# Row sums with the ones held still, a first root in two parts, high parts ahead of gate copies, and GpSimd scaling the last attention's probabilities

## What is computed

```python
# layer 0 and 1 of the first block: mod = silu(c) @ ada_w[i] + ada_b[i], six sections of 1024 each
h  = modulate(rmsnorm(x, norm1_g[i]), sh1, sc1)       # x*(1+sc1)+sh1
# layer 0: differential attention, 8 heads of 128, keys of context and x together (512)
p  = softmax(s[0]) - lam_full * softmax(s[1]);  o = p @ v
o  = rmsnorm(o, subln_g) * (1 - lam_init);      y = o.reshape(256, 1024) @ wo
# layer 1: short convolution
b_gate, c_gate, u = split(h @ w_in, 3);         y = (b_gate * conv3(c_gate * u)) @ w_out
# after each mixer: x = x + g1*y ; x = x + g2 * swiglu(modulate(rmsnorm(x), sh2, sc2))
# second block, layer 2: neighbourhood attention; layer 3: latent attention, 16 heads
pr = softmax(q @ k.T * 96**-0.5);  o = pr @ v;  y = (o * silu(z)) @ w_out
x  = h + sigmoid(rmsnorm(h) @ ple_w_gate) * (p @ ple_w_proj);  return rmsnorm(x, final_norm)
```

## Time and profile before

| what | value |
|---|---|
| time, median of 3 runs | 1090.65 us (1090.09 to 1091.9) |
| time of the profiled execution | 1092.87 us |
| span of its records | 1090.8 us |
| busy: TensorE matmul, weight load | 95%, 88% |
| busy: VectorE, ScalarE, GpSimd | 72%, 47%, 0% |
| mean granted TensorE clock | 0.982 of 2.4 GHz |

### The profile page before, as it was taken

The page is one execution under the profiler, slowest core; times in us unless marked ns, Lnnn a source line. Parts: engine busy times, 40 slices in busy tenths (PEclk is TensorE's granted clock), DMA queues, the critical chain, the costliest instruction groups (busy, mean ns, idle before and its releaser), DMA issues.

```text
span 1090.8 us, 18302 instructions
## 1 busy us (share of the span) xinstructions
PE 1035.3 (95%) x7740; PEld 960.9 (88%) x7740; DVE 790.3 (72%) x1184; ACT 509.4 (47%) x732; POOL 0.7 (0%) x6
## 2 busy tenths in 40 slices
PE   4899999799999999998999999999999999999895
PEld 2689875699999999998999999999987998997684
DVE  3689759668787887887986646568746568896665
ACT  3623238454434344424343444445347665457562
POOL 0000000000000000000000000000000000000000
PEclk9899999899999999999999999999999999999898
DMA  9769541038998987566746676564754053543130
GB/s 367 273 214 330 187 174 39 2 104 291 318 302 293 316 284 245 189 226 233 248 155 209 208 242 213 175 191 129 232 182 162 2 184 119 185 138 150 37 119 38
DMA packets 118592, 210.14 MB, mean 193 GB/s; under 512 B 4250, under 2 KB 82288, under 8 KB 118512
## 3 DMA queue, kind: packets, MB, share of 16 engines
q1 hardware_dynamic: 117764, 206.81, 55.9%
q10 hardware_dynamic: 748, 2.18, 0.5%
HBM read 207.92 MB, written 1.05 MB: 192 GB/s over the span
## 4 chain that ended last, share of the span: by engine, by line
PE 79%; DVE 12%; ACT 3%; issue 2%; DMA 1%; SPq 1%; DVEq 0%; ACTq 0%
PE PS L1625 12%; PE PS L1626 12%; PE PS L1627 12%; PE PS L1710 8%; PE PS L1729 8%; PE PS L1711 8%; DVE low L998 3%; PE PS L1636 3%; PE PS L1748 2%; PE PS L1749 2%; PE PS L1753 2%; PE PS L1843 1%; PE PS L1844 1%; DMA ada_raw<-in_ada_w 1%; PE PS L1916 1%
## 5 line engine op out<-in xcount | busy, mean ns | idle before, releaser
L998 DVE TENSOR_TENSOR low<-raw,high 128x2048 fp32r<-128x2048 f32 (+2 forms) x147 | 328.1, 2233 | 153.5 <-ACT high L585 153.1
L585 ACT ACTIVATE high<-raw 128x2048 fp32r<-128x2048 f32 (+2 forms) x147 | 273.1, 1866 | 226.0 <-PE PS L1627 111.2
L1710 PE MATMUL PS<-hH,high 128*128 128x258 f32 x896 | 221.8, 284 | 4.6 <-ACT high L585 1.9
L1711 PE MATMUL PS<-hL,high 128*128 128x258 f32 x896 | 220.3, 283 | 0.0
L1710 PEld LDWEIGHTS PS<-hH,high 128*128 128x128 f32 x896 | 169.8, 189 | 6.5 <-issue 2.9
L1711 PEld LDWEIGHTS PS<-hL,high 128*128 128x128 f32 x896 | 168.7, 188 | 0.1
L1729 PE MATMUL PS<-hH,low 128*128 128x258 f32 x896 | 126.3, 283 | 0.3
L1729 PEld LDWEIGHTS PS<-hH,low 128*128 128x128 f32 x896 | 115.6, 189 | 1.3 <-DVE low L998 1.3
L1625 PE MATMUL PS<-gH,high 128*128 128x256 f32 x352 | 98.5, 280 | 0.0
L1626 PE MATMUL PS<-gL,high 128*128 128x256 f32 x352 | 98.4, 280 | 0.0
L1627 PE MATMUL PS<-gH,low 128*128 128x256 f32 x352 | 98.2, 279 | 0.0
(11 more groups left out here) (325 smaller groups left out, 1945.8 us busy)
## 6 DMA issues: line engine op xcount, KB each, us to landing
raw<-in_ffn_w_in SPq DMA_DIRECT2D x44, 1024.0 KB, 6.4
ada_raw<-in_ada_w SPq DMA_DIRECT2D x82, 512.0 KB, 5.4
raw<-in_ffn_w_out SPq DMA_DIRECT2D x22, 1024.0 KB, 6.0
raw<-in_na_w_in SPq DMA_DIRECT2D x16, 1024.0 KB, 5.5
raw<-in_da_wqkv SPq DMA_DIRECT2D x12, 1024.0 KB, 8.8
raw<-in_sc_w_in SPq DMA_DIRECT2D x12, 1024.0 KB, 5.7
...
```

The source lines that it names most:

```text
L585: nc.scalar.activation(high[s][:, 0:width(u)], raw[s][:, 0:width(u)], ACT.Copy).then_inc(high_ready, 1)
L998: V_.tensor_tensor(low[s][:, 0:w], raw[s][:, 0:w], high[s][:, 0:w].bitcast(F), ALU.subtract).then_inc(low_dve, 1)
L1710: MM(PS[:, b + c, 0:SEQ + 2], high[s][w(j, c)], hH[:, j, 0:SEQ + 2], start=j == 0, stop=False)
L1711: MM(PS[:, b + c, 0:SEQ + 2], high[s][w(j, c)], hL[:, j, 0:SEQ + 2], start=False, stop=False)
```

## The change

1. **Sections 0 and 1**: `ada_acc` is turned by plain transposes, eight for each section into two banks (4, 5 and 6, 7), and one VectorE `tensor_reduce` for each adds the four tiles' rows. `sel2` goes.
2. **Sections 2 to 11**: the 32 columns of ones are stationary and 256 columns of `ada_acc` move, in four column tiles (four matmuls). ScalarE copies the 128x256 result to `sum_rows` (the tile `wide[3]`; `copy_rows`), and behind the next input unit TensorE turns it with two transposes (`turn_rows`) into bank 7, 5 or 6; VectorE takes it there (`section_turned`).
3. **The first root**: heads of rounds 0 to 11 are rooted in three steps inside rounds 13, 14 and 15, their blocks scaled, turned and split ahead of the rest; the last block of four heads follows, and TensorE turns it behind the first output unit. `newton` is split into `root_guess`, `root_series` and `root_closed`, the operations being the same.
4. **The convolution's input**: ScalarE calls `behind` of unit 3j before it waits for the gate copy.
5. **The last attention**: ScalarE's `gated_high` comes ahead of the exponentials; VectorE keeps the reciprocals, and GpSimd does the 32 scalings.

Left out of the diff: declarations of semaphores, `sel2`, and the splitting of `newton`.

```diff
@@ -187,6 +187,13 @@
+def rows_bank(u, first):
+
+    if u < first["ffn0"]:
+return 7
+    return 6 if first["sc_in"] <= u < first["ffn1"] else 5
@@ -563,6 +573,11 @@
     nc.gpsimd.memset(cond[:, :, :], 0.0).then_inc(consts_ready, 1)
+    for h in range(16):
+        pool.wait_ge(sums_inverted, h + 1)
+        for t in range(TT):
+            ins = nc.gpsimd.tensor_scalar(E2[:, h % 4, t, :], E2[:, h % 4, t, :], rsum[:, 2 * h + t:2 * h + t + 1], None, ALU.mult)
+        ins.then_inc(probs_scaled, 1)
@@ -586,6 +601,12 @@
+
+    def copy_rows(u):
+
+        if u in reduce_at:
+            seen.next(rows_made)
+            nc.scalar.activation(sum_rows[:, :], bank(7, SEQ), ACT.Copy).then_inc(rows_copied, 1)
@@ -662,6 +683,7 @@
         behind(first["da_q"] + j)
+        copy_rows(first["da_q"] + j)
     def da_exp(i):
@@ -677,6 +699,7 @@
             nc.scalar.activation(V[:, tt, 512 * nb:512 * nb + 512], bank(V_BANK[nb][tt]), ACT.Copy).then_inc(vz_copied, 1)
+        copy_rows(ua + 1)
         behind(ua + 1)
@@ -721,6 +744,7 @@
             ua = u0 + (3 * i - 1 if i else 0)
+            copy_rows(ua)
             seen.next(a_taken)
@@ -741,13 +765,14 @@
         u = first["sc_in"] + 3 * j
+        behind(u)
         seen.next(c_taken)
...
         ins.then_inc(c_copied, 1)
-        behind(u)
         behind(u + 1)
         behind(u + 2)
+        copy_rows(u + 2)
         act.wait_ge(conv_staged, j + 1)
@@ -918,11 +943,11 @@
         turned(2 * p + 1)
+        if p % 2 == 0 and p:
+            gated_high(p // 2 - 1)
         if p + 2 < 8:
...
             exps(2 * p + 5, False)
-        if p % 2 == 0 and p:
-            gated_high(p // 2 - 1)
     behind(first["mla_kvb"] + 2)
@@ -977,18 +1002,30 @@
-    def section(g):
-
+    turning = []
+
+    def section(u):
+
+        turning.append((reduce_at[u], rows_bank(u, first)))
+
+    def section_turned():
+
+        if not turning:
+            return
+        g, b = turning.pop()
         layer, part = divmod(g, 6)
...
         sections_done[0] += 1
-        b = cols[:, NROWS + 8 * g:NROWS + 8 * g + 8]
+        by_column = "p (j h) -> p j h"
+        src = bank(b, SEQ).rearrange("p (h j m) -> p j h m", h=2, j=4)[:, :, :, 0]
+        here = mod[:, g, :].rearrange(by_column, h=2)
+        beta = cols[:, NROWS + 8 * g:NROWS + 8 * g + 8].rearrange(by_column, h=2)
         if part in (SCALE1, SCALE2):
             at, _ = ROWS["norm1_g" if part == SCALE1 else "norm2_g"]
-            link(V_.scalar_tensor_tensor(mod[:, g, :], bank(7, KC), 1.0, b, ALU.add, ALU.add))
+            link(V_.scalar_tensor_tensor(here, src, 1.0, beta, ALU.add, ALU.add))
             V_.tensor_tensor(mod[:, g, :], mod[:, g, :], cols[:, at + 8 * layer:at + 8 * layer + 8], ALU.mult).then_inc(section_taken, 1)
         else:
-            V_.tensor_tensor(mod[:, g, :], bank(7, KC), b, ALU.add).then_inc(section_taken, 1)
+            V_.tensor_tensor(here, src, beta, ALU.add).then_inc(section_taken, 1)
@@ -998,8 +1035,9 @@
     def sections(u):
+        section_turned()
         if u in reduce_at:
-            section(reduce_at[u])
+            section(u)
@@ -1083,7 +1131,10 @@
         b = cols[:, NROWS + 8 * g:NROWS + 8 * g + 8]
-        src = PS[:, (7, 0)[g], 0:16].rearrange("p (c m) -> p m c", m=2)
+        four_rows = PS[:, 4 + 2 * g:6 + 2 * g, :].rearrange("p b (c j m) -> p (b c) m j", c=4, j=4)[:, :, 0:2, :]
+        src = (nwt, var)[g][:, 0:16].rearrange("p (c m) -> p c m", m=2)
+        link(V_.tensor_reduce(src, four_rows, AX.X, ALU.add))
+        src = src.rearrange("p c m -> p m c")
         if g == 0:
@@ -1174,31 +1225,50 @@
+    def da_scaled(t, b):
+        heads = XN[:, t, 512 * b:512 * b + 512].rearrange("p (h e) -> p h e", h=4)
+        k = 8 * t + 4 * b
+        V_.tensor_tensor(heads, heads, rst[:, k:k + 4].unsqueeze(2).to_broadcast([P, 4, P]), ALU.mult).then_inc(xn_ready, 1)
+
+    def da_low(t, b):
+        sl = (slice(None), slice(4 * b, 4 * b + 4), slice(t * P, (t + 1) * P))
+        direct_low(oL[sl], oH[sl], GROUP_BANK[2 * t + b], cols[:, at:at + 1])
...
     da_max(2)
+    section_turned()
     for i in range(16):
...
             da_max(i + 3)
+        if i == 13:
+            v.wait_ge(sq_ready, 12)
+            link(V_.tensor_scalar(var[:, 0:12], ssq[:, 0:12], 1.0 / P, EPS, ALU.mult, ALU.add))
+            root_guess(var[:, 0:12], rst[:, 0:12], nwt[:, 0:12])
+        if i == 14:
+            root_series(nwt[:, 0:12], poly[:, 0:12])
+        if i == 15:
+            root_closed(rst[:, 0:12], nwt[:, 0:12], poly[:, 0:12])
+            da_scaled(0, 0)
+            da_scaled(1, 0)
         seen.next(made_v)
...
             split(first["da_v"] + 3 + RING)
+    da_scaled(0, 1)
+    da_low(0, 0)
+    da_low(1, 0)
     v.wait_ge(sq_ready, 16)
-    inverse_root(0, 16, P)
-    for t, b in BY_HALF:
-        heads = XN[:, t, 512 * b:512 * b + 512].rearrange("p (h e) -> p h e", h=4)
-        k = 8 * t + 4 * b
-        V_.tensor_tensor(heads, heads, rst[:, k:k + 4].unsqueeze(2).to_broadcast([P, 4, P]), ALU.mult).then_inc(xn_ready, 1)
-    for t, b in BY_HALF:
-        sl = (slice(None), slice(4 * b, 4 * b + 4), slice(t * P, (t + 1) * P))
-        direct_low(oL[sl], oH[sl], GROUP_BANK[2 * t + b], cols[:, at:at + 1])
+    inverse_root(12, 16, P)
+    da_scaled(1, 1)
+    da_low(0, 1)
+    da_low(1, 1)
@@ -1549,10 +1620,7 @@
         seen.next(exp_ready)
-        link(V_.reciprocal(rsum[:, 2 * h:2 * h + 2], esum[:, 2 * h:2 * h + 2]))
-        for t in range(TT):
-            ins = V_.tensor_scalar(E2[:, h % 4, t, :], E2[:, h % 4, t, :], rsum[:, 2 * h + t:2 * h + t + 1], None, ALU.mult)
-        ins.then_inc(probs_scaled, 1)
+        V_.reciprocal(rsum[:, 2 * h:2 * h + 2], esum[:, 2 * h:2 * h + 2]).then_inc(sums_inverted, 1)
@@ -1636,21 +1704,37 @@
+    turning = []
+
+    def turn_rows():
+
+        if not turning:
+            return
+        b = rows_bank(turning.pop(), first)
+        seen.next(rows_copied)
+        claim(b)
+        transposes(b, [(h * P, P, sum_rows[:, h * P:(h + 1) * P]) for h in range(2)]).then_inc(section_made, 1)
+        owed(section_taken, b)
...
+        turn_rows()
         if u not in reduce_at:
...
         claim(7)
-        owed(section_taken, 7)
-        for c in range(KC):
-            last = MM(PS[:, 7, c:c + 1], ada_acc[g % 2][:, c * P:(c + 1) * P], ones[:, 0:1], start=True, stop=True)
-        last.then_inc(section_made, 1)
-
-    def output_groups(s, order):
-
-        seen.n[split_low.name + "/freed"] = seen.n[split_low.name]
+        for j in range(4):
+            last = MM(PS[32 * j:32 * j + 32, 7, 0:SEQ], ones[:, 0:32], ada_acc[g % 2][:, j * SEQ:(j + 1) * SEQ],
+                      start=True, stop=True, tile_position=(0, 32 * j))
+        last.then_inc(rows_made, 1)
+        owed(rows_copied, 7)
+        turning.append(u)
+
+    def output_groups(s, order, first_of=True):
+
+        if first_of:
+            seen.n[split_low.name + "/freed"] = seen.n[split_low.name]
         for t, b in order:
@@ -1819,15 +1903,13 @@
     for g in range(2):
-        b = (7, 0)[g]
-        pe.wait_ge(acc_copied, g + 1)
-        claim(b)
-        for c in range(KC):
-            if c == 4:
-                pe.wait_ge(acc_half, g + 1)
-            last = MM(PS[:, b, 2 * c:2 * c + 2], ada_acc[g][:, c * P:(c + 1) * P], sel2[:, :], start=True, stop=True)
+        for n in range(2):
+            b = 4 + 2 * g + n
+            pe.wait_ge((acc_copied, acc_half)[n], g + 1)
+            claim(b)
+            last = transposes(b, [(c * P, P, ada_acc[g][:, (4 * n + c) * P:(4 * n + c + 1) * P]) for c in range(4)])
         last.then_inc(section_made, 1)
-        owed(section_taken, b)
+        owed(section_taken, b - 1, b)
@@ -1916,17 +1999,19 @@
         owed(o_taken, 7)
-    output_groups(xn_ready, BY_HALF)
-
-    def feature_out(u0, per_unit):
+    output_groups(xn_ready, BY_HALF[:3])
+
+    def feature_out(u0, per_unit, last_group=False):
         for k in range(4):
+            if last_group and k == 1:
+                output_groups(xn_ready, BY_HALF[3:], False)
             if per_unit[k]:
...
-    feature_out(first["da_out"], (2, 0, 2, 0))
+    feature_out(first["da_out"], (2, 0, 2, 0), True)
```

18 lines of the change are left out of this document (13 added, 5 removed).

## The result

| what | before | changed |
|---|---|---|
| median of the runs timed together (4 each) | 1091.07 us | 1065.99 us (1065.78 to 1067.14) |
| ratio, 95% interval | | 0.9773 (0.9756 to 0.979) |
| profiled execution, span | 1092.87, 1090.8 us | 1066.09, 1064.3 us |

The changed kernel is 25.1 us faster; 24.3 were forecast, 1066.4 against 1066.0. That it came so close is partly luck: of the five terms one rested on a wrong reason, and inside it a gain of 4.8 us and a loss of 2.3, neither of them forecast, made up nearly the 3.0 that were.

A forecast was written before the change was run, and what follows sets the result against it. TensorE, busy 95%, was taken as the bound: savings count where it executes the removed work or waits. Terms 1.0 + 6.7 + 11.0 + 2.6 + 3.0 = 24.3 off 1090.65 gave 1066.4 us, range 1060 to 1074.

The forecast's parts named there:

- The cross-check from TensorE's side: Convolution's input: 7.2 us slack, 2.85 from half clock and two sections at 0.8 make 11.6 us saved.
- The 1.1 for the section ahead of the first scores: First attention's inputs: the section ending them saves 1.1 us, as maxima and exponentials follow directly.
- 207.6: First root: the first output unit starts at about 207.6 us, 3.7 earlier, before 1.0 back for the fourth block.
- Rival (b): Half clock returns in full behind the convolution's input and first root: 8.1 and 0.2 saved, 1071.7 us; chance 0.17.
- Freed of the scalings VectorE takes the maxima at once: Last attention: without scalings VectorE starts pair 7's maxima 0.9 us earlier, part of 2.4 us saved.
- the formula 0.5 + 4t: Last attention: a round's time in us when GpSimd's scaling time t exceeds the limit of 0.87 us.
- Rival (e): Last attention: GpSimd's scalings set the rounds, change slower; break-even 1.7 us a scaling, 1099 us at 2.0; chance 0.03.
- Rival (a): Last attention: GpSimd takes about 1.3 us a scaling, rounds of 5.7 us, total 1079.4 us; chance 0.10.
- Rival (c): Sections 2 to 11: tiled sums save only 0.4 us each or turning awaits the copy, total 1070.4 us; chance 0.09.
- Rival (f): Convolution's input: the wait only moves, VectorE waiting for a round's second high part, total 1077 us; chance 0.02.
- Rival (d): Start or last attention: clock never falls at one or two places, saving 3.7 and 5.2, 1061.5 us; chance 0.10.
- Rival (g): Last attention: one-time start-up of GpSimd's first scaling; 8 us long it costs 6, total 1072 us; chance 0.04.

The follow-up runs named there:

- e5: The changed kernel with sections 0 and 1 summed by 16 matmuls with two moving columns again: 1067.64 us.
- e4: The changed kernel with eight one-column matmuls for each of sections 2 to 11 again, no copy and no transposes: 1073.37 us.
- e7: The kernel before with one edit, ScalarE's high part of unit 3j ahead of the gate copy in the convolution's input: 1079.25 us.
- e3: The changed kernel with one root of 16 heads behind round 15 again, all four blocks turned ahead of the output units: 1069.28 us.
- e2: The changed kernel with ScalarE's gate copy ahead of all three high parts again in the convolution's input: 1077.5 us.
- e10: The changed kernel, early roots of twelve heads kept, but TensorE turns all four blocks ahead of the first output unit: 1071.0 us.
- e1: The changed kernel with the last attention's 32 scalings on VectorE again, gated_high still ahead of the exponentials: 1064.05 us.
- e8: The kernel before with one edit, gated_high ahead of the exponentials in the last attention, VectorE scaling: 1087.13 us.
- e9: The changed kernel with gated_high behind the exponentials again, GpSimd still scaling: 1070.51 us.
- e11: The changed kernel with no edit, run again beside the version with VectorE's scalings: 1066.56 us.

## Why the prediction was right, and where it was not

| term | forecast | measured | by |
|---|---|---|---|
| sections 0 and 1 | 1.0 (0.8 to 3.7) | 1.65; 0.9 in the traces at split 10 | e5 |
| sections 2 to 11, with the 1.6 in the convolution | 8.3 | 7.4 | e4 |
| convolution's input, order alone | 9.4 | 10.0 | trace of e7 |
| first root | 2.6 (0.2 to 3.3) | 3.3; 4.3 in the traces | e3; leads |
| last attention | 3.0 (1.5 to 5.2) | 2.55 | leads |

Parts that were taken out of the changed kernel need not add up to its gain: e2 also lost the sums' 1.6.

**Point 3 was right for its reason.** VectorE's rounds are 17.6 and 17.0 us, its splits wait for nothing, the first output unit follows without a gap, and the stretch at half clock is gone. The cross-check from TensorE's side, 7.2 of slack, 2.85 of clock and 1.6 of sums, made 11.6, and 11.6 is what the lead grew by. I had then taken the rounder 11.0. Only who leads was read wrongly: TensorE is busy for the whole 37.50 us, so it sets the rounds now and not VectorE.

**Point 2 was right, with its sizes nearly so.** A section now costs the stream 0.57 for the tiled step, 0.2 at the steps' ends and 0.14 + 0.1 for the turning, the 1.0 forecast; the four in a clean stream give 0.85 each, not 0.8. The 1.1 for the section ahead of the first scores I cannot confirm.

**Point 1** is not told apart from its forecast. `dH` starts at 35.52 where 35.4 was said, and the lead at splits 0 and 10 is 1.5, so in this pair of executions the 1.5 is passed on. But e5 puts what the sums alone are worth between 0.9 and 1.65, and the half-clock stretch of the start is 3.4 us here where it was 10.2 before; it differs between executions of one program, so it cannot be put down to the change.

**Point 4's upper bound, 3.3, failed** by the traces. I gave the first output unit as 3.7 earlier and took 1.0 off for the fourth block. It is 4.35 earlier against output 15 (7.20 behind it in the earlier trace rows), and the lead at the next splits is no lower than at the unit itself. The steps that failed were "207.6", which priced the turning partly at the half clock of the old trace, and the 1.0: the fourth block's root and scaling lie beside a unit of TensorE's work, its high and low part beside the next, and only four transposes are in the stream (some 0.4 us from 208.97), which the clock returned to the first matmuls pays. The half clock that the text read at 211.27 is in neither of the rows that it names, but in the stretch from 205.40 shown above. Rival (b), half clock coming again at this place, did not come about; e3 and e10 show it where the last block is awaited.

**Point 5 had the total and the wrong cause.** The step was "Freed of the scalings VectorE takes the maxima at once". e1 shows that VectorE does so with the scalings too, e8 that ScalarE's order alone gives rounds of 3.97 and 5.0 in the trace, and e9 that GpSimd alone loses 1.9. What made the maxima late was VectorE's wait for `oH`, which the trace of the kernel before has twice in its later rounds:

```profile
1009.16 0.69 DVE L1565 TENSOR_TENSOR oL<-X,oH 128x512 fp32r<-128x512 f32 x1 [1.92 <-ACT oH L606]
...
1017.83 0.69 DVE L1565 TENSOR_TENSOR oL<-X,oH 128x512 fp32r<-128x512 f32 x1 [1.92 <-ACT oH L606]
```

The second stands two microseconds ahead of the maxima of pair 7 that the text had read, and the sum gave nothing for it, nor for the edit that takes it away. The second step, GpSimd's "0.5", was 0.91, above its range (0.32 to 0.76) and above the limit of 0.87 that the text itself gave. For 0.91 the formula 0.5 + 4t makes a round of 4.1; measured were 3.97 and 4.39 in turn, 4.18. So the edit on ScalarE brought 4.8, that on GpSimd cost 2.3, and their sum happened to be near my 3.0. Rival (e), slower through GpSimd, had the right mechanism at half its price: at 0.91 us it takes back half of what the other edit in its part gives, at 1.7 it would have decided the whole.

Rival (a) is out at 0.91, short of its 1.3. Rival (c) was refuted by the start-to-start of 0.57 and by e4's 0.85 a section; rival (f) by 0.1 us of waiting in twelve splits. Rival (d) came about as to the clock, which no longer falls at the last attention's end, but the gain there was 2.55 and not its 5.2. One sign of being wrong did show, a half-clock stretch that was new, at the first scores; e11 is the same kernel without it. Rival (g), a start-up of GpSimd: in the changed kernel the first scaling starts at 968.77, 0.25 us after the start of the reciprocals it needs. The 5.95 us that the Trainium skill (GPSIMD Engine Reference, Instruction dispatch) gives for the first call of a freshly loaded kernel is not seen here, at least not on the path.
